# Two expert chunks of a loop pass loaded as 112 rows and twice 8 rows

## The chip, the cores and the metric

The kernel runs on one core of a Trainium2 chip. The metric is the device time of one execution in microseconds (us). A core has a matrix engine (TensorE, PE in the profile; its weight loads are PEld), VectorE (DVE), ScalarE (ACT), GpSimd (POOL) and SyncE (SP, which here issues nearly all loads), and 16 DMA engines that move data between the chip's memory and the core's on-chip memory of 128 partitions.

## The reference, cut to what matters

Two blocks work on 256 tokens of width 1024 in float32. The first has attention, retention, attention to a memory, and at its end a mixture of 32 experts; the second has two layers, each with a feed-forward part, token mixers and another feed-forward part. The change touches how the experts' weights are loaded:

```
def expert_block(args):
    toks, e = args
    xb = t_pad[toks]
    return (jax.nn.silu(xb @ w1[e]) * (xb @ w3[e])) @ w2[e]
```

Every expert has three matrices of 1024x512, 6 MB in all. Which tokens go to which expert is data, but the kernel streams the weights of all 32 experts in a fixed order.

## The kernel before, in words

The experts' weights come as 192 chunks of 1 MB: 128 rows of 8192 bytes, one for each partition. An expert is six chunks: four for the gate and up matrices, two for the down matrix. Four experts make a team, a team is served in one turn of 24 chunks (`TURN`), and two turns make a pass over 48 chunks. The first pass is written out (two turns, with `prev` equal to None); the others are a loop, `Fori(0, last_pair)` on SP at L2075 and on PE at L719. Eight teams of four experts make four passes, so the loop runs three times here.

The chunks go to slots of 8192 bytes per partition in one large on-chip buffer, the tile `ring` (and, for some slots, `more`). `expert_place` (L452) gives the slot of the j-th chunk and how many times it has been filled; in the loop sixteen slots are used in rotation, three fills of each per pass. Every slot has a semaphore `e_land[s]`; a load of a slot increments it by 16 when it has fully landed.

- SP (L2075 to L2078): for each of the 48 chunks of a pass it waits on `e_used`, which PE increments with the last matmul on a chunk, so that the slot is free, and then issues one load, in `expert_chunk` (L2042 to L2047).
- PE: `chunk_of` (L636) waits until the slot's semaphore has reached the count of its fills so far, and `turn` (L661) then runs the matmuls of the chunk: at L683 those of the gate and up matrices, at L702 those of the down matrix, with a transpose at L692 between. At the end of a turn L712 scatters the team's result. ACT (L753, L757, L760) and DVE (L868, L727) work on what lies between.
- Behind the loop SP goes on in `layer_loads` (L930) with the weights of the first feed-forward part of the second block, in tiles of 128 rows of 12288 bytes (tile memory `ring` again, input `in_wf`). For the first eight tiles, L943 waits until PE is through with the slots that the tile overwrites, L938 until the tile two before has landed, and L939 issues the load.
- ACT copies tile 0 and tile 1 at L974 (`whu`) as they land, in this order, then casts the transposed tokens (L1256), and PE starts the feed-forward part at L1183 when that is there.

All these loads are issued on one queue (q1 in the profile), in the order of the program.

Of the kernel before, what the change touches and what calls it, by code (L numbers as in the profile page):

```python
# [30 lines left out]
ESLOTS = 16  # L31
# [32 lines left out]
TURN = 6 * TEAM  # L64
# [32 lines left out]
def build(nc, d_x, d_mem, d_w1, d_we, d_wf, d_w2, d_cT1, d_row1, d_wr, d_cT2, d_row2, d_ln, d_tab, d_bias, d_out):  # L97
    ctx = ExitStack()
    with ctx:
# [42 lines left out]
        slot = [ring[:, s * CH:(s + 1) * CH] for s in range(SLOTS)]  # L142
# [67 lines left out]
        def block2(n):  # L210
            return n + 12 if n < 4 else n - 4 if n < 16 else n
# [15 lines left out]
        def sem(name):  # L227
            return ctx.enter_context(nc.semaphore(name))
# [15 lines left out]
        e_land = [sem(f"e_land{i}") for i in range(ESLOTS + EXTRA)]  # L244
# [126 lines left out]
        def head_rows(T, blk, first, n):  # L371
            return [T[first:first + n, blk, tok(i)] for i in range(NT)], T[first:first + n, blk, :]

        units1 = []
        for h in range(AH):
            rows = 64 * (h % 2)
            q, _ = head_rows(qkT, h // 2, rows, 64)
# [10 lines left out]
        for h in range(4):  # L388
            at_q, kv = [0, 2, 1, 3][h], h // 2
            q, _ = head_rows(qkT2, block2(at_q // 2), 64 * (at_q % 2), 64)  # L390
# [4 lines left out]
        for n in range(8):  # L395
            h, m = n // 2, n % 2
            q, _ = head_rows(qkT2, block2(3 + 2 * (n // 4)), 32 * (n % 4), 32)
# [4 lines left out]
        for h in range(4):  # L402
            at_q, kv = [0, 2, 1, 3][h], h // 2
            q, _ = head_rows(qkT2, block2(8 + at_q // 2), 64 * (at_q % 2), 64)
# [4 lines left out]
        for h in range(BH):  # L409
            q, _ = head_rows(qkT2, block2(10 + h), 0, BQ)  # L410
# [41 lines left out]
        def expert_place(j):  # L452

            if ESLOTS <= j < ESLOTS + EXTRA:
                return j, 1
            r = j if j < ESLOTS else j - EXTRA
            return e_slot[r % ESLOTS], r // ESLOTS + 1
        dense_slot = [(D_AT + c) % SLOTS for c in range(DENSE2)]
        OUT_ORDER = (0, 3, 2, 1)
        BANKS_W = (6, 0, 1, 2)  # L460
# [149 lines left out]
        def pe_moe(pe, tokens):  # L610
# [25 lines left out]
            def chunk_of(prev, t, j):  # L636

                n = t * TURN + j
                if prev is None:
                    s, fills = expert_place(n)  # L640
                    pe.wait_ge(e_land[s], fills * 16)
                else:
                    s, fills = expert_place(2 * TURN + n)
                    pe.wait_ge(e_land[s], (prev * (2 * TURN // ESLOTS) + fills) * 16)
                return slot[s].rearrange("p (k q n) -> p k q n", k=2, q=4)

            def weights_T(it):
# [13 lines left out]
            def turn(prev, t):  # L661
# [5 lines left out]
                for e, part in TEAM_ORDER:  # L667
                    if part == "u":
                        for c in range(4):
                            if e == 0:  # L670
                                if c == 1:
                                    pe.wait_ge(n_ok, 2)
                                    gather(it, 2)
                                if c == 2:
                                    gather(it, 3)
                                pe.wait_ge(m_xg, it * 4 + (c + 1))
                                if c == 2:
                                    weights_T(it)
                            w = chunk_of(prev, t, j)
                            for kk in range(2):  # L680
                                k = 2 * c + kk
                                for q in range(4):
                                    ins = pe.matmul(bank[4 + e % 2][q * CAP:(q + 1) * CAP, 0:2 * P],  # L683
                                                    xg[:, k, e * CAP:(e + 1) * CAP], w[:, kk, q],
                                                    start=(k == 0), stop=(k == KD - 1), skip_group_check=True)
                            ins.then_inc(e_used, 1)
                            j += 1
                        continue
# [8 lines left out]
                    for c in range(2):  # L697
                        w = chunk_of(prev, t, j)
                        for kk in range(2):
                            k = 2 * c + kk  # L700
                            for q in range(4):
                                ins = pe.matmul(bank[6][q * CAP:(q + 1) * CAP, 0:2 * P],  # L702
                                                hTe[:, e % 2, k * CAP:(k + 1) * CAP], w[:, kk, q],
                                                start=(k == 0), stop=(k == 3), skip_group_check=True)
                        ins.then_inc(e_used, 1)
                        j += 1
# [223 lines left out]
        def layer_loads(sp, last_pair):  # L930
            for p in range(2):
                sp.sem_inc(f_land[p], 16)
            for l in range(LAYERS):
                for f in range(2):
# [6 lines left out]
                    for v in range(FSLOTS):  # L941
                        if g == 0:
                            sp.wait_ge(e_used, last_pair * (2 * TURN) + max(  # L943
                                j + 1 for j in range(2 * TURN) if expert_place(2 * TURN + j)[0] in chunks_in(v)))
                        elif f == 0 and last_tile[(v + RING0) % FSLOTS] >= FT - 2:
                            sp.wait_ge(f_dn, g * (FT + 1))
                        elif f == 0:
                            sp.wait_ge(wl_ok, g * FFN_W + (2 * last_tile[(v + RING0) % FSLOTS] + 2))
                        else:
                            sp.wait_ge(d_used, l * DENSE2 + (DENSE1 + 1 + max(last_dense[s] for s in chunks_in(v))))  # L950
                        tile(v, v % 2)
# [1049 lines left out]
        def _(sp):  # L2001
# [24 lines left out]
            for t in (before, ones, iota, rel, desc, rope):  # L2026
                n = int(np.prod(t.shape[1:]))
# [14 lines left out]
            def expert_chunk(pair, j, place):  # L2042

                e, c = TEAM_CHUNKS[j % TURN]
                src = d_we[((pair % (TEAMS // 2)) * 2 * TEAM + (j // TURN * TEAM + e)) * 6 + c]
                s, _ = expert_place(place)
                sp.dma_start(slot[s], src).then_inc(e_land[s], 16)  # L2047

            by_slot = {expert_place(j)[0]: j for j in range(ESLOTS + EXTRA)}
            for free in (12, 13, 0, 1, 2, 3, 10, 11, 14, 15, 4, 16, 17, 5, 6, 8, 7, 9, 18, 19, 20):  # L2050
                if free < SLOTS1:
                    sp.wait_ge(d_used, DENSE1 - SLOTS1 + free + 1)
                elif free < SLOTS1 + 2:
                    sp.wait_ge(d_used, DENSE1 - 1 + free - SLOTS1)
                elif free < SLOTS:
                    sp.wait_ge(d_used, V1[-1] + 1)
                elif free < SLOTS + 2:
                    sp.wait_ge(o_ok, AH)
                elif free < ESLOTS:
                    sp.wait_ge(o_ok, UNITS1)  # L2060
                elif free < ESLOTS + 2:
                    sp.wait_ge(t_ps, 34)
                elif free == ESLOTS + 2:
                    sp.wait_ge(d_used, DENSE1)
                elif free == ESLOTS + 3:
                    sp.wait_ge(sumsq, 4)
                else:
                    sp.wait_ge(r_ps, 1)
                expert_chunk(0, by_slot[free], by_slot[free])
            used = 2 * TURN  # L2070
            for j in range(ESLOTS + EXTRA, used):
                sp.wait_ge(e_used, j - ESLOTS - EXTRA + 1 if j < 2 * ESLOTS + EXTRA else j - ESLOTS + 1)
                expert_chunk(0, j, j)
            last_pair = load_pairs(sp)
            with sp.Fori(0, last_pair) as prev:  # L2075
                for j in range(used):
                    sp.wait_ge(e_used, prev * used + (used - ESLOTS + j + 1))
                    expert_chunk(prev + 1, j, used + j)  # L2078
# [1078 lines left out]
```

## Time and profile before

| | |
|---|---|
| median of 3 runs | 1750.41 us |
| the three runs | 1749.85, 1750.41, 1752.44 us |
| the profiled execution's own time | 1750.45 us |
| its span, first to last instruction | 1748.7 us |
| mean granted TensorE clock, share of full speed | 0.946 |
| PE busy | 92% of the span |
| chain that ended last | PE 64%, DMA 11%, SP's queue 9% |

The span is what the trace shows; the device time is 1.75 us longer than it. Times in the trace count from the first instruction. The page cuts the span into 40 slices of 43.7 us; the expert stage lies from about 265 to 703 us, slices 7 to 16. "DMA share" is the mean busy share of the 16 DMA engines. It can exceed 1 a little, because a packet's recorded time overlaps the next one's by some nanoseconds, and by much in a very short window, where a packet counts with its whole time in the window in which it starts.

### The profile page before, as it was taken

To read this page: it belongs to the slowest core of one execution; us is meant where nothing else is said; L and a number is where in the kernel's file an instruction comes from. 1 tells how busy PE (TensorE), PEld (TensorE's weight loads), DVE (VectorE), ACT (ScalarE), POOL (GpSimd) and SP (SyncE) were. 2 spreads that over 40 slices of the span, in tenths; PEclk is the share of its full clock that TensorE was granted. 3 is DMA by queue.
4 is the path that set the end of the run, shared out by engine and by line. 5 is a ranking of instruction groups with operands and counts; after the bars stand their busy time and mean duration, and the time that the engine had idled before them with its cause. 6 is when DMAs were issued, how large, how long until landed. Compare 5 with 4: busy or idle time off the path is not lost.

```text
span 1748.7 us, 27045 instructions
## 1 busy us (share of the span) xinstructions
PE 1609.7 (92%) x10486; PEld 1219.6 (70%) x10497; DVE 957.6 (55%) x1493; ACT 622.5 (36%) x961; POOL 226.6 (13%) x241
## 2 busy tenths in 40 slices
PE   8999999777777776999999999999999999999998
PEld 6788985333323332788887788888888887788886
DVE  5675543111111110677776767677767766677767
ACT  5464431100010000443443643444344443653332
POOL 0232110000000000100133321001110133411000
PEclk9999999888767877999999999999999999999999
DMA  9515489999999999955445055533854534055511
GB/s 396 195 63 169 172 338 386 426 426 427 424 427 426 425 426 427 369 213 190 175 176 193 1 222 199 180 108 133 330 181 168 216 127 186 25 220 191 195 43 49
DMA packets 61100, 421.47 MB, mean 241 GB/s; under 512 B 7024, under 2 KB 16080, under 8 KB 17360
## 3 DMA queue, kind: packets, MB, share of 16 engines
q1 hardware_dynamic: 59280, 409.13, 59.7%
q10 hardware_dynamic: 1728, 11.03, 1.7%
q8 instruction: 68, 1.11, 0.2%
q14 instruction: 24, 0.20, 0.0%
HBM read 419.08 MB, written 1.05 MB: 240 GB/s over the span
## 4 chain that ended last, share of the span: by engine, by line
PE 64%; DMA 11%; SPq 9%; DVE 6%; issue 4%; POOL 3%; ACT 2%; DVEq 0%; ACTq 0%; POOLq 0%
PE bank L1162 17%; PE bank L1205 12%; DMA ring<-in_we 9%; SPq L2047 9%; PE bank L1164 9%; PE bank L2198 6%; PE bank L2224 2%; PE bank L2127 2%; PE bank L683 2%; PE bank L1545 2%; POOL x L1056 2%; DMA ring<-in_wf 2%; PE bank L1192 1%; PE bank L1183 1%; PE bank L1151 1%
## 5 line engine op out<-in xcount | busy, mean ns | idle before, releaser
L1162 PE MATMUL bank<-xhl,whu 128*128 128x512 f32 x1280 | 451.8, 396 | 0.0
L1164 PE MATMUL bank<-xhl,wlu 128*128 128x256 f32 x1280 | 357.5, 279 | 0.0
L1162 PEld LDWEIGHTS bank<-xhl,whu 128*128 128x128 f32 x1280 | 240.3, 188 | 57.8
L1164 PEld LDWEIGHTS bank<-xhl,wlu 128*128 128x128 f32 x1280 | 241.1, 188 | 3.3
L979 DVE TENSOR_TENSOR wlu<-ring,whu 128x2048 fp32r<-128x2048 f32 x84 | 192.5, 2292 | 43.9 <-ACT whu L974 43.9
L974 ACT ACTIVATE whu<-ring 128x2048 fp32r (+1 forms) x88 | 167.2, 1902 | 3.5 <-DMA ring<-in_wf 3.5
L979 DVE TENSOR_TENSOR wld<-ring,whd 128x1024 fp32r<-128x1024 f32 x80 | 98.6, 1233 | 113.4 <-ACT whd L974 113.4
L683 PE MATMUL bank<-ring,xg 128*32 128x256 f32 x1424 | 115.0, 466 | 39.1 <-DMA ring<-in_we 39.1
L974 ACT ACTIVATE whd<-ring 128x1024 fp32r (+1 forms) x80 | 84.8, 1060 | 128.5 <-PE bank L1205 128.5
L1272 ACT ACTIVATE sg<-sg 128x256 f32<-128x256 f32 x80 | 33.5, 418 | 265.8 <-DVE sg L1351 265.8
L683 PEld LDWEIGHTS bank<-ring,xg 128*32 128x32 f32 x1424 | 46.2, 126 | 99.4 <-DMA ring<-in_we 68.1
L2198 PE MATMUL bank<-ring_r,xTh 128*128 128x512 f32 x384 | 109.8, 397 | 4.6 <-DVE ring_r L514 2.5
L868 DVE TENSOR_TENSOR hmid<-hact,bank 128x128 f32<-128x128 f32 x32 | 9.2, 288 | 186.1 <-ACT hact L753 186.1
L702 PE MATMUL bank<-ring,hTe 128*32 128x256 f32 x832 | 76.4, 505 | 31.9 <-DMA ring<-in_we 21.6
L987 POOL TENSOR_TENSOR wlu<-ring,whu 128x512 fp32r<-128x512 f32 x16 | 21.2, 1355 | 586.3 <-ACT whu L974 556.1
L727 DVE COPY yg<-bank 32x256 f32<-32x256 f32 x64 | 27.2, 424 | 122.1 <-PE bank L702 121.6
L1205 PE MATMUL bank<-whd,hh 128*128 128x512 f32 x288 | 91.2, 398 | 0.0
L1205 PE MATMUL bank<-whd,hl 128*128 128x512 f32 x288 | 91.0, 397 | 0.0
L1205 PE MATMUL bank<-wld,hh 128*128 128x512 f32 x288 | 90.7, 396 | 0.0
L1056 POOL TENSOR_TENSOR x<-x,ln 128x512 f32<-128x512 f32 x40 | 63.5, 1600 | 204.5 <-DVE wlu L979 192.0
L2198 PEld LDWEIGHTS bank<-ring_r,xTh 128*128 128x128 f32 x384 | 71.3, 188 | 22.5 <-issue 3.2
L514 DVE TENSOR_TENSOR ring_r<-ring,ring_r 128x2048 fp32r<-128x2048 f32 x26 | 59.6, 2291 | 49.4 <-ACT ring_r L506 49.4
(349 smaller groups left out, 2777.4 us busy)
## 6 DMA issues: line engine op xcount, KB each, us to landing
ring<-in_we SPq DMA_DIRECT2D x141, 1024.0 KB, 26.9
ring<-in_wf SPq DMA_DIRECT2D x88, 1536.0 KB, 6.4
ring<-in_w SPq DMA_DIRECT2D x52, 1024.0 KB, 5.0
more<-in_we SPq DMA_DIRECT2D x51, 1024.0 KB, 25.8
ring<-in_w SPq DMA_DIRECT2D x32, 256.0 KB, 3.7
ln<-in_ln ACTq DMA_DIRECT2D x6, 1024.0 KB, 5.9
bias<-in_bias ACTq DMA_DIRECT2D x2, 2048.0 KB, 7.3
bias<-in_bias SPq DMA_DIRECT2D x1, 2048.0 KB, 20.4
```

What stands on the lines that cost most here:

```text
L514: ins = eng.tensor_tensor(slot_r[n % SLOTS1][:, part], slot[n % SLOTS1][:, part], high1[n % 2][:, part].bitcast(F32), ALU.subtract)
L683: ins = pe.matmul(bank[4 + e % 2][q * CAP:(q + 1) * CAP, 0:2 * P], xg[:, k, e * CAP:(e + 1) * CAP], w[:, kk, q], start=(k == 0), stop=(k = ...
L702: ins = pe.matmul(bank[6][q * CAP:(q + 1) * CAP, 0:2 * P], hTe[:, e % 2, k * CAP:(k + 1) * CAP], w[:, kk, q], start=(k == 0), stop=(k == 3 ...
L974: act.activation(dst[:], ring[:, bass.ds(ring_tile(t) + first, D if down else 2 * D)], ACT.Copy).then_inc(wh_ok, 1)
L979: eng.tensor_tensor(dst[:], ring[:, bass.ds(ring_tile(t) + first, D if down else 2 * D)], src[:].bitcast(F32), ALU.subtract).then_inc(done, 1)
L1056: ins = pool.tensor_tensor(x[:, i, cols], x[:, i, cols], ln[:, n // 4, cols], (ALU.mult, ALU.add)[n // 4])
L1162: pe.matmul(into[:].rearrange("p (a s) -> p a s", a=2), whu[p][:, cols], xhl[:, :, k], start=(k == 0), stop=False, skip_group_check=True)
L1164: ins = pe.matmul(into[:, 0:S], wlu[p][:, cols], xh[:, k], start=False, stop=(k == KD - 1), skip_group_check=True)
L1205: ins = pe.matmul(bank[2 * i + c][:], v[p][:, tok(i)], w[p][:, c * 512:(c + 1) * 512], start=False, stop=False, skip_group_check=True)
L1545: ins = pe.matmul(bank[BANKS_W[2 * i + h]][:], v[:, tok(i)], w[:, kk, h * 512:(h + 1) * 512], start=(pos == 0 and kk == 0 and m == 0), sto ...
L2047: sp.dma_start(slot[s], src).then_inc(e_land[s], 16)
L2198: ins = pe.matmul(bank[banks[2 * i + h]][:], v[:, k, tok(i)], w[:, kk, h * 512:(h + 1) * 512], start=(k == 0 and m == 0), stop=(k == KD - ...
```

## The change

In the loop, and there only, chunks number 22 and 46 of a pass are loaded by three instructions in place of one: rows 0 to 111, rows 112 to 119 and rows 120 to 127. Each of the three increments the slot's semaphore by 16, so such a fill counts 48. The wait of PE is adapted: `turn_lands` gives, for chunk n of a loop pass, the slot, how much its semaphore rises per pass, and the count for the first pass. Chunk 22 is the first of the two down chunks of the last expert of the first turn, and chunk 46 the same of the second turn. The same bytes are loaded to the same places in the same order of chunks.

```diff
+        UNEVEN = (22, 46)
+
+        def extra_land(j):
+
+            return 32 if j in UNEVEN else 0
+
+        def turn_lands(j):
+
+            s, fills = expert_place(2 * TURN + j)
+            same = [q for q in range(2 * TURN) if expert_place(2 * TURN + q)[0] == s]
+            return s, 16 * len(same) + sum(map(extra_land, same)), fills * 16 + sum(extra_land(q) for q in same if q <= j)
+
...
                 else:
-                    s, fills = expert_place(2 * TURN + n)
-                    pe.wait_ge(e_land[s], (prev * (2 * TURN // ESLOTS) + fills) * 16)
+                    s, every, first_at = turn_lands(n)
+                    pe.wait_ge(e_land[s], prev * every + first_at)
...
                 s, _ = expert_place(place)
-                sp.dma_start(slot[s], src).then_inc(e_land[s], 16)
+                if place >= 2 * TURN and j in UNEVEN:
+                    sp.dma_start(slot[s][0:112], src[0:112]).then_inc(e_land[s], 16)
+                    for r in (112, 120):
+                        sp.dma_start(slot[s][r:r + 8], src[r:r + 8]).then_inc(e_land[s], 16)
+                else:
+                    sp.dma_start(slot[s], src).then_inc(e_land[s], 16)
```

## Rows read from the trace of the kernel before

**Rows 1.** Busy tenths in 40 slices of the span, from the page.
```profile
PE   8999999777777776999999999999999999999998
...
PEclk9999999888767877999999999999999999999999
DMA  9515489999999999955445055533854534055511
GB/s 396 195 63 169 172 338 386 426 426 427 424 427 426 425 426 427 369 213 190 175 176 193 1 222 199 180 108 133 330 181 168 216 127 186 25 220 191 195 43 49
```

**Rows 2.** Stretches: us, PE busy, PEld, DVE, ACT, POOL, clock, DMA share, GB/s.
```profile
320.00:440.00 120.00, 86.44 (x872) 38.35 (x876) 15.11 (x45) 10.99 (x34) 0.00 (x0) 0.80 1.01 426
560.00:680.00 120.00, 88.92 (x868) 37.78 (x860) 15.07 (x44) 11.07 (x34) 0.00 (x0) 0.77 1.01 426
730.00:800.00 70.00, 70.00 (x366) 59.29 (x365) 50.04 (x61) 26.69 (x25) 0.00 (x0) 1.00 0.67 246
```

**Rows 3.** Waits from 320 to 700: who for whom, total us, times, longest.
```profile
PEld bank L683 <- DMA ring<-in_we: 68.1, 43, 2.8
...
PE bank L683 <- DMA ring<-in_we: 39.1, 41, 2.3
```

**Rows 4.** The DMA view of the stretch from 285 to 700 us.
```profile
q1 hardware_dynamic: 24115, 176.20, 100.7%
q8 instruction: 30, 0.49, 0.4%
...
ring<-in_we SPq DMA_DIRECT2D x120, 1024.0 KB, 27.1
more<-in_we SPq DMA_DIRECT2D x38, 1024.0 KB, 25.9
```

**Rows 5.** Chain that ended last, 640 to 712 us: start, length, what.
```profile
647.39 27.70 DMA ring<-in_we
675.09 0.04 issue
675.13 1.83 PE bank L683 x16
...
678.96 28.19 DMA ring<-in_wf
707.15 0.02 issue
707.17 1.92 ACT whu L974
709.09 0.03 issue
709.11 0.61 ACT xhl L1256
709.72 0.14 issue
709.85 5.98 PE bank L1183 x48
```

**Rows 6.** DMA share of all 16 engines in short stretches around 700 us.
```profile
699.00:699.50 0.50, 0.00 (x0) 0.00 (x0) 0.00 (x0) 0.00 (x0) 0.00 (x0) 1.00 1.06 451
699.50:700.00 0.50, 0.09 (x4) 0.10 (x8) 0.00 (x0) 0.00 (x0) 0.00 (x0) 1.00 0.81 344
700.00:700.50 0.50, 0.50 (x12) 0.32 (x16) 0.00 (x0) 0.00 (x0) 0.00 (x0) 1.00 0.81 344
700.50:701.00 0.50, 0.48 (x12) 0.00 (x0) 0.00 (x0) 0.00 (x0) 0.00 (x0) 1.00 0.52 221
...
703.50:704.00 0.50, 0.50 (x3) 0.26 (x2) 0.38 (x1) 0.47 (x1) 0.00 (x0) 1.00 0.52 221
```

**Rows 7.** ACT's timeline where the first two feed-forward tiles have landed.
```profile
703.52 1.91 ACT L974 ACTIVATE whu<-ring 128x2048 fp32r<-128x2048 f32 x1 [1.72 <-DMA ring<-in_wf]
```

**Rows 8.** The line of the expert loads, and SP's timeline of two tile issues.
```profile
L2047 SPq FUSED_REGOPS  x144: 46/46/139, 320.0 to 670.5; - x144
L2047 SPq DMA_DIRECT2D ring<-in_we x141: 340/1892/5898, 198.9 to 670.6; - x141
...
703.58 8.29 SPq L939 DMA_DIRECT2D ring<-in_wf  x3
761.09 0.34 SPq L957 DMA_DIRECT2D ring<-in_wf  x1
```

**Rows 9.** Packets that start within 0.2 us after two issues, DMA view.
```profile
DMA packets 9, 0.11 MB, mean 553 GB/s; under 512 B 0, under 2 KB 0, under 8 KB 0
...
DMA packets 10, 0.12 MB, mean 614 GB/s; under 512 B 0, under 2 KB 0, under 8 KB 0
```

## The prediction

> **What bounds the kernel now.** I read the page's slices first. PE is busy nine tenths nearly everywhere, but in slices 8 to 16 it falls to six or seven tenths while the DMA engines stand at nine and move 424 to 427 GB/s [rows 1]. That is the expert stage. The stretches say the same: DMA share 1.01 and 426 GB/s, PE busy 86 to 89 of 120 us [rows 2]. The waits name what PE lacks there: its weight loads at L683 wait 68.1 us for landings of `in_we`, its matmuls 39.1 us [rows 3]. Between 285 and 700 us the queue carries 158 chunks, each landing 26 to 27 us after its issue [rows 4]. A chunk of 1.049 MB at 426 GB/s takes 2.46 us, so some eleven are in flight: what counts is when the DMA engines get to the end of the queue, not when SP issues. The chain that ended last goes the same way: a chunk's 27.7 us, PE on it, then the 28.19 us of a feed-forward tile behind the experts in the same queue, ACT's copy and cast, and PE's L1183 at 709.85 us [rows 5]. From there PE is busy without a gap (70.00 of 70.00 us between 730 and 800, at clock 1.00) and the DMA share is down to 0.67 [rows 2]. So what the stage gives or loses up to 709.85 us goes one to one to the end, and nothing else the loads do matters much.
>
> **The finer reading** is that the 16 engines don't finish together. A landing needs all of them. Near 700 us the last expert chunk and tiles 0 and 1 are in the queue, and tile 2 is issued only when tile 0 has fully landed (L938). The DMA share is 1.06 until 699.5, falls to 0.81, and stands at 0.52 from 700.5 to 704 [rows 6]. Half of the engines have nothing left, while the other half still works: it ends tile 0 at 703.5 (ACT's copy starts at 703.52 [rows 7]) and tile 1 at 707.15 [rows 5]. The early half was through with tile 1 at about 700.0, the middle of the fall. It is thus 7.1 us ahead of the slowest late one, and the landings, PE and the end go by the late half. What makes half of them late I can show in part: 30 fetches of instructions of 16 KB went through the same engines in that stretch, with 0.4% of 16 engines for 415 us [rows 4], 27 us. Spread over eight engines these are 3.3 us each, about half of the 7.1.
>
> **The change part by part.** All is priced against the profiled execution, 1750.45 us (span 1748.7 plus 1.75), which is 0.04 us from the median of 1750.41.
>
> (a) *Rows taken from engines.* Every engine has 8 of a chunk's 128 rows. A row takes 2.46 / 8 = 0.308 us on its engine. Loading 112 rows leaves 7 on each of the sixteen. Two pieces of 8 rows must then put 16 rows somewhere. If a piece uses eight engines, and both pieces the same eight, these have 9 rows and the other eight 7. No DMA of this trace shows a piece of 8 rows, so I bound it. At one end the pieces fall on the early half: the late half has one row less per uneven chunk. At the other end they fall on the late half and it has one more. SP's register instruction runs 144 times from 320 us on [rows 8], three passes of 48, so there are 6 uneven chunks: -1.85 or +1.85 us. Wider ends (all rows on one engine; an even spread) are rivals below.
>
> (b) *Which half.* One view bears on it. Tile 2 is issued at 703.58 us, when one half is idle, and 10 packets start from 0.92 to 1.12 us behind the issue; the busy half, at one 12 KB packet in 0.46 us (2.46 x 1.5 / 8), starts 3 or 4 of these, so 6 or 7 of the idle eight are at work by then. At 761.09 us a tile is issued with all sixteen idle [rows 8], and between 0.91 and 1.11 us 9 of the sixteen start [rows 9] (first row 762.0 to 762.2, second row 704.5 to 704.7). Were engines served in no order, about 4.5 of the idle eight would have started; were the idle half the last served, about one. It looks like the half that is served first. A piece for eight engines would naturally take the first ones. This is two launches and an inference, so it moves my odds and proves nothing.
>
> The Trainium skill says this outright: the page "DMA: Bandwidth & Descriptors", section "Why a DMA increments its semaphore by 16 and not by 1", has a load use the largest number of engines up to 16 that divides its rows, the lowest-numbered ones. By that 112 rows use 16 engines and 8 rows the lowest 8; with (b) the sum would be -1.85 us. No row here numbers the engines.
>
> (c) *Does the whole -1.85 arrive?* The early half gets 1.85 us later, so its lead shrinks from 7.1 by 3.7 to 3.4 us. It stays ahead, so the late half still sets each landing, and nothing takes its place. Tile 0, tile 1, the transposes and L1183 all hang on landings of the same queue and move together. PE's sequence before L1183 (last chunk, scatter, transposes) starts from a landing as well. I take all of it: -1.85.
>
> (d) *Twelve more loads on SP.* Issues of L2047 take 0.34 to 5.90 us, 1.89 in the middle [rows 8]; an issue of 0.34 us is one into a free queue, as at 761.09. Twelve cost SP 4.1 us at the least, 22.7 at the middle value and 71 at the most. I take zero for the end: SP runs 26 to 27 us ahead of the landings [rows 4], two issues of one chunk can eat at most 11.8 us of this, and the queue refills before the next uneven chunk 24 chunks (59 us) later. If that cover were gone, the 22.7 us would count. What stands behind the two issues on SP is the next chunk's wait and load, with the same cover. POOL and ACT issue nothing here.
>
> (e) *Semaphore writes and PE's waits.* Each extra piece adds writes of a few bytes on the early half only, which has 3.4 us to spare. PE's wait is a register instruction as before; even 0.05 us more for the 18 waits on the two slots would be 0.9 us, and PE idles before most of them for a landing [rows 3]. Zero, at most +0.9.
>
> Sum: 1750.45 - 1.85 = **1748.6 us**, 0.11% less. A measurement of this kernel can tell about 0.2%, 3.5 us, from no change (the runs of before lie 2.6 us apart), so the likeliest verdict is the same.
>
> **The rivals.** *The pieces fall on the late half* (place: the queues of that half; price 6 x 0.308; it decides if the first-served eight are the late ones). 1750.45 + 1.85 = 1752.3, slower than before. For it: only that (b) is thin. 0.14.
>
> *Nothing moves.* If the rows of a piece are cut so that all 16 engines share them, each engine again has 8 rows' worth: 1750.4. The same if tile 1's time were set by PE instead; against that stands the wait of ACT for the landing [rows 7]. 0.09.
>
> *All 8 rows of a piece on one engine.* It gets 7 + 16 rows in place of 8, 15 x 6 x 0.308 = 27.7 us more, less its lead of 7.1 if it is an early one: 1771. Against it: large loads here spread over all engines. 0.03.
>
> *The small pieces cost by the piece.* If SP or the queue spends 1.9 us on each whatever its size and the cover of (d) doesn't hold, 12 x 1.89 = 22.7 us: 1773. Against it: eleven chunks in flight. 0.04. The Trainium skill's page "DMA: Bandwidth & Descriptors", section "Rules for kernel authors", speaks for this one: small transfers are to be coalesced, and under 64 KB one pays mostly overhead (a piece is 64 KB); its fixed cost of about 2.0 us (section "Anatomy of one DMA") would give an estimate of 24 us.
>
> *A larger gain*, over 3.5 us, if late landings also cost elsewhere, as in SP's or PE's waits behind them: 0.04. The forecast itself has 0.66.
>
> **How the numbers follow.** The forecast alone gives 1747.0 to 1750.2, the spread of the runs around 1748.6. To reach 8 in 10 the range must take in "nothing moves" and the late half at 1752.3: 1746.8 to 1752.5. Faster by over 0.2% (under 1746.9): the larger gain and the edge of the forecast, 0.11. Slower by over 0.2% (over 1753.9): both costly rivals and the edge of the late-half one, 0.09. Same: 0.80.
>
> **What the profile after would show.** Right: under `in_we` six loads of 112 rows and twelve small ones; around 698 us the half-idle stretch (share near 0.5) shorter by about 3.7 us, and L1183 at about 708.0. Rival late half: the half-idle stretch longer by 3.7 us, L1183 at 711.7. Nothing moves: L1183 at 709.85. Small pieces by the piece: DMA share under 1 behind the uneven chunks, landings well under 26 us. The prediction is wrong if L1183 doesn't move by 1.85 us, or if it does and the end doesn't follow.

## The result and the profile after

The changed kernel takes 1790.76 us (median of 6 runs, 1783.9 to 1794.25), the kernel before beside it 1751.5 (6 runs, 1749.85 to 1755.32): ratio 1.0219, 95% interval 1.0201 to 1.0238. It is slower by 39 us, where 1.85 us less were forecast. The profiled execution took 1790.11 us with a span of 1788.3, against 1748.7 before.

The page first, its slices. Those of before are [rows 1].

```profile
PE   9999999767757757699999999999999999999998
PEclk9999999877767678799999999999999999999999
DMA  9515499999999999885436126534654445055511
GB/s 397 194 48 180 174 372 378 426 389 422 387 367 426 367 362 426 285 314 189 166 145 230 71 68 274 180 136 165 262 202 177 165 187 189 1 225 187 187 59 47
DMA packets 61196, 421.47 MB, mean 236 GB/s; under 512 B 7120, under 2 KB 16176, under 8 KB 17456
```

The DMA engines stand at nine in the expert stage as before, but five of its slices move only 362 to 389 GB/s where every one moved 424 or more. So the engines are as busy and do less. The bytes are the same 421.47 MB. Before, the page counted 61100 packets, 7024 of them under 512 B: there are 96 more now, all of them tiny. In e1 below, twelve additional loads of 128 rows leave 192 more (7216 in all), 16 each, one for every engine. Here twelve additional loads leave 96, 8 each: a piece of 8 rows uses eight engines, as part (a) of the prediction supposed.

Where the time went stands in the stretches (the columns are those of [rows 2]).

```profile
380.00:394.00 14.00, 9.40 (x92) 2.85 (x84) 0.85 (x2) 0.75 (x2) 0.00 (x0) 0.62 1.01 425
394.00:404.00 10.00, 4.74 (x38) 1.62 (x34) 1.14 (x3) 1.58 (x5) 0.00 (x0) 0.50 1.01 243
404.00:420.00 16.00, 14.44 (x97) 7.26 (x97) 3.42 (x11) 0.74 (x2) 0.00 (x0) 0.71 1.01 424
320.00:440.00 120.00, 86.82 (x843) 38.12 (x843) 14.95 (x44) 10.54 (x33) 0.00 (x0) 0.74 1.01 411
440.00:560.00 120.00, 83.46 (x796) 37.72 (x796) 14.21 (x42) 10.32 (x32) 0.00 (x0) 0.73 1.01 389
560.00:680.00 120.00, 78.51 (x710) 32.21 (x710) 13.16 (x39) 9.86 (x30) 0.00 (x0) 0.70 1.01 380
```

There is a hole of about 10 us, from 394 to 404. The rate drops from 425 to 243 GB/s and comes back, and all the while the share is 1.01. Five more follow, one for each uneven chunk. The DMA views of the first two stretches count the packets.

```profile
DMA packets 818, 5.95 MB, mean 425 GB/s; under 512 B 93, under 2 KB 93, under 8 KB 93
...
DMA packets 351, 2.43 MB, mean 243 GB/s; under 512 B 54, under 2 KB 54, under 8 KB 54
...
q1 hardware_dynamic: 351, 2.43, 101.5%
```

In 14 us 16 engines carried 725 large packets, 0.31 us of an engine each. In the 10 us of the hole they carried 297, at full share, which is 0.54 us each. If eight engines had been slowed and the others had waited idle, the share would have dropped. It didn't: nearly all engines spent longer on each packet. The trace's packet records say the same one by one: from 380 to 394 us all but one of 724 packets of 8192 bytes took 0.309 us, and of the 162 that start from 396 to 402 us none took less than 0.475.

PE's granted clock is 0.50 in the hole. PE mostly waits there, and the DMA engines are full all the while, so a slower PE is not what holds the loads up.

The uneven chunk of this hole was issued at 371 us, 23 us earlier. SP's timeline shows its three loads, and line L2062 gives all twelve small ones.

```profile
371.38 0.36 SPq L2060 DMA_DIRECT2D ring<-in_we  x1
371.92 5.95 SPq L2062 DMA_DIRECT2D ring<-in_we  x2
...
L2062 SPq DMA_DIRECT2D ring<-in_we x12: 295/1987/5415, 371.9 to 705.7; - x12
```

The queue is some 26 us long [rows 4], so the hole sits where the queue reaches the uneven chunk, not where SP issues it. The issues of the small loads last 1.99 us in the middle, as other issues into this full queue do ([rows 8], 1.89), and the page still has the loads of `in_we` landing 27.1 us after their issue in the middle. SP is not what is late. What is late is the landing: of the waits, here 320 to 740 us, matmuls and weight loads at L714 (L702 before) have grown most. They waited 21.6 and 28.7 us for landings of `in_we` before.

```profile
PEld bank L695 <- DMA ring<-in_we: 65.9, 40, 3.7
...
PE bank L714 <- DMA ring<-in_we: 53.6, 35, 3.8
PEld bank L714 <- DMA ring<-in_we: 50.4, 27, 3.9
PE bank L695 <- DMA ring<-in_we: 38.7, 40, 3.1
```

The chain that ended last now ends its expert part with chunk 47, the one behind the last uneven chunk and held up in the same queue:

```profile
708.82 30.58 DMA ring<-in_we
...
739.44 1.92 PE bank L714 x16
...
749.55 5.47 PE bank L1195 x45
```

L1195 is L1183 of before. It starts at 749.55 us in place of 709.85 [rows 5], 39.7 us later, and the span is 39.6 us longer. All of the loss arises before this point and nothing is won back behind it; from 750 on PE is busy without a gap as before. Tiles 0 and 1 have landed when ACT's copies of them start, at 703.52 [rows 7] and 707.17 [rows 5] before, and both are 39.5 us later:

```profile
743.06 1.91 ACT L986 ACTIVATE whu<-ring 128x2048 fp32r<-128x2048 f32 x1 [0.91 <-DMA ring<-in_wf]
746.71 1.91 ACT L986 ACTIVATE whu<-ring 128x2048 fp32r<-128x2048 f32 x1 [1.74 <-DMA ring<-in_wf]
```

Shared over six uneven chunks the loss is 6.6 us each, for a chunk that took 2.46. The engines don't lose alike. By the packet records the packets of 8192 bytes between 270 and 760 us took 35.3 us per engine beyond 0.309 us each, before 2.6: the mean engine lost 32.7 us, and the last one, for which every landing waits, 39.5. Shortly before tile 0 has landed only two of sixteen still work (a share of 0.12):

```profile
739.00:742.00 3.00, 1.87 (x16) 0.60 (x16) 0.60 (x2) 0.60 (x2) 0.00 (x0) 0.65 0.12 49
```

### The profile page after: what moved, and what is told of

Read it like the earlier page. It is cut to its first block, busy times and chain, and to the rows that moved or that the text cites. A ratio compares the mean times of both kernels' runs of the same rounds, so it can differ in the third digit from the quotient of the medians.

```text
span 1788.3 us, 27087 instructions
## 1 busy us (share of the span) xinstructions
PE 1615.8 (90%) x10486; PEld 1223.6 (68%) x10497; DVE 957.8 (54%) x1493; ACT 622.1 (35%) x961; POOL 226.4 (13%) x241
## 2 busy tenths in 40 slices
DMA packets 61196, 421.47 MB, mean 236 GB/s; under 512 B 7120, under 2 KB 16176, under 8 KB 17456
## 4 chain that ended last, share of the span: by engine, by line
PE 63%; DMA 11%; SPq 10%; DVE 6%; issue 4%; POOL 3%; ACT 2%; DVEq 0%; ACTq 0%; POOLq 0%
PE bank L1174 17%; PE bank L1217 11%; SPq L2064 9%; PE bank L1176 8%; DMA ring<-in_we 7%; PE bank L2215 6%; DMA more<-in_we 4%; PE bank L2241 2%; PE bank L2144 2%; PE bank L1557 2%; PE bank L695 2%; POOL x L1068 2%; PE bank L1204 1%; PE bank L1195 1%; PE bank L1163 1%
## 5 line engine op out<-in xcount | busy, mean ns | idle before, releaser
L695 PE MATMUL bank<-ring,xg 128*32 128x256 f32 x1424 | 110.5, 453 | 38.7 <-DMA ring<-in_we 38.7
L714 PE MATMUL bank<-ring,hTe 128*32 128x256 f32 x832 | 81.7, 532 | 58.8 <-DMA ring<-in_we 53.6
L714 PEld LDWEIGHTS bank<-ring,hTe 128*32 128x32 f32 x832 | 29.1, 139 | 99.1 <-DMA ring<-in_we 50.4
## 6 DMA issues: line engine op xcount, KB each, us to landing
ring<-in_we SPq DMA_DIRECT2D x135, 1024.0 KB, 27.1
```

Of the source, the lines that this page charges most:

```text
L714: ins = pe.matmul(bank[6][q * CAP:(q + 1) * CAP, 0:2 * P], hTe[:, e % 2, k * CAP:(k + 1) * CAP], w[:, kk, q], start=(k == 0), stop=(k == 3 ...
```

## The experiments

The first theories were these. **N**: loads cost by their number, three for one. **B**: the balance of rows over engines is worse than I took it. **P**: it matters which rows a load writes. P comes in two forms: P1 blames the load of 112 rows, P2 the pieces of 8 neighbouring rows. **H**, for e11, says that only a crowded queue is disturbed, and that loads by themselves go by their bytes. Each experiment but e11 touches chunks 22 and 46 alone, or adds loads right behind them. The diffs of e1, e2, e3, e6, e12 and e13 are against the changed kernel, the others against the kernel before; `...` marks lines left out. The kernel before, run beside them, had medians of 1750.85 us (for e1, e2, e3 and e6, 15 runs) and 1752.15 (e7 to e10, 7 runs, 1749.34 to 1753.04), and 1751.28 in one run (e11 to e13).

### e1: three loads of all 128 rows

```diff
-                    sp.dma_start(slot[s][0:112], src[0:112]).then_inc(e_land[s], 16)
-                    for r in (112, 120):
-                        sp.dma_start(slot[s][r:r + 8], src[r:r + 8]).then_inc(e_land[s], 16)
+                    for a, b in ((0, 1024), (1024, 1536), (1536, 2048)):
+                        sp.dma_start(slot[s][:, a:b], src[:, a:b]).then_inc(e_land[s], 16)
```

> Chunks 22 and 46 of a loop pass are loaded in three instructions as in the change, but cut by columns (1024, 512 and 512 of 2048) with all 128 rows in each. Theory P (places: the cut by rows takes engines off their own share of partitions, and several then write through the same port): no slow packets, end within 3 us of before, about 1751. Theory N (number: three loads and 48 counts on one semaphore in place of one load cost by themselves): about as slow as the change, 1785 to 1790. Theory B (balance: the two small pieces overload one half of the engines): within 3 us of before too, since the cut by columns keeps all 16 engines equal.

Measured: 1752.78 us (1750.73 to 1753.82), ratio 1.0007, interval 0.9997 to 1.0016. The same. It has as many loads, as much semaphore work and the same waits as the change, and no hole:

```profile
394.00:404.00 10.00, 5.67 (x67) 2.27 (x68) 2.59 (x8) 1.76 (x5) 0.00 (x0) 0.97 1.02 424
```

N falls. Terms (d) and (e) of the prediction, additional issues and semaphore writes, are too small to be measured. It is the cut by rows that costs.

### e2: 112 and 16 rows

```diff
-            return 32 if j in UNEVEN else 0
+            return 16 if j in UNEVEN else 0
...
-                    sp.dma_start(slot[s][0:112], src[0:112]).then_inc(e_land[s], 16)
-                    for r in (112, 120):
-                        sp.dma_start(slot[s][r:r + 8], src[r:r + 8]).then_inc(e_land[s], 16)
+                    for a, b in ((0, 112), (112, 128)):
+                        sp.dma_start(slot[s][a:b], src[a:b]).then_inc(e_land[s], 16)
```

> The same chunks as 112 rows and one piece of 16 rows, which all 16 engines can share; no piece of 8 rows is left. Theory P1 (the 112 rows do it, 7 consecutive rows to an engine): dips of the DMA rate as in the change, 4 to 7 us lost at each of the six chunks, end 1775 to 1790. Theory P2 (the pieces of 8 rows do it, eight engines on a few neighbouring partitions): little is left, end under 1760. Theory B: no loss, 1751.

Measured: 1792.68 us (one run), 41.8 over before. The page counts 7120 packets under 512 B, 96 more than before, so each load of 16 rows uses all sixteen engines. There is no piece of 8 rows here, and the time is that of the change, so neither the pieces of 8 nor the balance that they make is the main cause: B falls as such.

### e3: halves, rows 0 to 63 and 64 to 127

```diff
-            return 32 if j in UNEVEN else 0
+            return 16 if j in UNEVEN else 0
...
-                    sp.dma_start(slot[s][0:112], src[0:112]).then_inc(e_land[s], 16)
-                    for r in (112, 120):
-                        sp.dma_start(slot[s][r:r + 8], src[r:r + 8]).then_inc(e_land[s], 16)
+                    for a, b in ((0, 64), (64, 128)):
+                        sp.dma_start(slot[s][a:b], src[a:b]).then_inc(e_land[s], 16)
```

> The same chunks as two halves of 64 rows, 4 rows to each of the 16 engines. Theory P: 64 neighbouring partitions reach only half of the ports, so while a half is written the engines share them by two and packets take about twice 309 ns: at least 2.5 us lost for each of the six chunks, end over 1765. Theories N and B: no loss for balance; N gives two thirds or half of the change's 39 us.

Measured: 1783.57 us (one run), 32.7 over before, 5.5 us a chunk. 64 and 64 is as even a cut as there is, and still dear. Both show the hole, e2 in the first row and e3 in the second:

```profile
394.00:404.00 10.00, 4.02 (x41) 1.66 (x45) 0.85 (x2) 1.02 (x3) 0.00 (x0) 0.62 0.99 286
```

```profile
394.00:404.00 10.00, 3.90 (x38) 1.47 (x41) 1.14 (x3) 1.41 (x5) 0.00 (x0) 0.65 1.01 283
```

### e12: halves again, every second row

The question that remains behind e3 is whether a load of 64 rows is dear, or these 64 rows are. This one writes the even rows with one load and the odd rows with the other.

```diff
-            return 32 if j in UNEVEN else 0
+            return 16 if j in UNEVEN else 0
...
-                    sp.dma_start(slot[s][0:112], src[0:112]).then_inc(e_land[s], 16)
-                    for r in (112, 120):
-                        sp.dma_start(slot[s][r:r + 8], src[r:r + 8]).then_inc(e_land[s], 16)
+                    for r in (0, 1):
+                        sp.dma_start(slot[s][r:127 + r:2], src[r:127 + r:2]).then_inc(e_land[s], 16)
```

> Chunks 22 and 46 as two loads of 64 rows, but even rows and odd rows instead of the upper and the lower half. The number of loads, rows and bytes is that of the 64 and 64 run (1783.6). Theory P: each load now reaches all ports, so engines crowd less, end between 1755 and 1775. If only the count of rows per engine matters: 1783 again.

Measured: 1751.51 us, the kernel before beside it 1751.28 (one run each). Expected were 1755 to 1775; it costs nothing at all. The stretch has its full rate:

```profile
394.00:404.00 10.00, 6.88 (x66) 2.31 (x65) 1.93 (x5) 2.04 (x6) 0.00 (x0) 0.67 1.01 428
```

e3 and e12 load the same bytes with as many loads of as many rows, and lie 32 us apart. Which rows go together in a load decides. That is P. (The two also group the source rows differently; e7, e8 and e11 leave the source alone and show the same.)

### e13: only one of the two chunks uneven

```diff
-        UNEVEN = (22, 46)
+        UNEVEN = (22,)
```

> The change with chunk 22 alone cut up (three chunks in all instead of six). Each uneven chunk costs by itself, 39 / 6 = 6.5 us: end near 1770. If the cost came from the first of them or from the adapted waits: 1785 or more.

Measured: 1770.66 us (one run), 19.4 over before, 6.5 for each of three chunks where the change has 6.6 for each of six. The costs add up chunk by chunk. No one place in the pass is to blame.

### e9 and e10: the 112 rows and the 16 rows alone, as spare loads

These and the next two kernels keep all chunks of before whole and add loads behind chunks 22 and 46. They fill slot 20, which is not in use then, have a semaphore of their own, and nobody reads what they bring. PE waits for nothing new. SP waits, ahead of the next spare loads and once in `layer_loads`, until the last ones have landed.

```diff
...
+            SPARE = {22: [(0, 112, 1)], 46: [(0, 112, 1)]}
...
+                    if j in SPARE:
+                        rows = SPARE[j]
+                        sp.wait_ge(spare_in, prev * 48 + 32 * (j == 46) + 16 * (j == 22))
+                        for n_, (a, b, step) in enumerate(rows):
+                            sp.dma_start(slot[20][a:b:step], d_we[0][0:(b - a + step - 1) // step]).then_inc(spare_in, 16)
...
```

> The kernel before plus one spare load of 112 rows behind chunks 22 and 46, no piece of 8 rows anywhere. The bytes alone are 7 rows more per engine, 6 x 7 x 0.308 = 12.9 us, end 1763. Theory P1: slow packets as in the change, 20 to 35 us more on top, 1785 to 1800. Theory P2: 1763 and packets of 309 ns.

Measured: 1805.25 us (one run), 53.1 over before, and more than P1's 1785 to 1800. The bytes account for 6 x 0.875 x 2.46 = 12.9 us of it. The other 40.2 us, 6.7 a load, are as much as the change lost in all (39.3). Its hole:

```profile
394.00:404.00 10.00, 5.10 (x54) 2.08 (x50) 1.14 (x3) 1.52 (x5) 0.00 (x0) 0.67 1.02 289
```

e10 has `SPARE = {22: [(0, 16, 1)], 46: [(32, 48, 1)]}` in its place.

> The kernel before plus one spare load of 16 neighbouring rows behind chunks 22 and 46; the bytes alone are 1 row more per engine, 1.85 us, end 1752.3. Theory P1: that and nothing more. Theory P2 (small pieces on few partitions): some us more, 1755 to 1765.

Measured: 1759.04 us (one run), 6.9 over before, of which bytes are 1.85. Sixteen neighbouring rows cost 0.8 us a load beyond their bytes. 1759 lies in the range of P2, not in P1's "nothing more": the small neighbouring pieces cost something too. But it is an eighth of what a load of 112 rows costs, so that one is the dear one of the change's loads.

### e7 and e8: four pieces of 8 rows, apart or neighbouring

Both have four spare pieces of 8 rows behind each of the two chunks, 24 in all. In e7 a piece takes every fourth of 32 rows, in e8 eight neighbours. Both read the same source rows.

```diff
+            SPARE = {22: [(0, 29, 4), (1, 30, 4), (2, 31, 4), (3, 32, 4)], 46: [(32, 61, 4), (33, 62, 4), (34, 63, 4), (35, 64, 4)]}
```

```diff
+            SPARE = {22: [(0, 8, 1), (8, 16, 1), (16, 24, 1), (24, 32, 1)], 46: [(32, 40, 1), (40, 48, 1), (48, 56, 1), (56, 64, 1)]}
```

> The kernel before, all chunks whole, plus four spare loads of 8 rows of 8192 bytes behind chunks 22 and 46 of each loop pass, into a slot that nobody reads then; a piece takes every fourth of 32 rows (partitions r, r+4, ... r+28 of the lower 64), so that each row falls to another group of four partitions. 24 rows more for the eight engines of such pieces, 24 x 0.308 = 7.4 us. Theory P: no slow packets. If those eight are the early half, which is 7.1 us ahead, the end moves by 0 to 2.5 us (1751 to 1753); if they are the late half, by 7.4 (1758). Theory N (by the piece): 24 pieces cost as much as the change's 12 or more, over 1780.

> As the run before, with the same sources and sizes, but each piece goes to 8 neighbouring partitions. Only the place of the rows differs. Theory P2 (pieces of 8 neighbouring rows clog): slow packets behind each uneven chunk, end clearly over that of the run before, by 5 to 20 us. Theory P1 (only the 112 rows do it) and the reading that the source in memory is what collides: the same as the run before within 2 us.

Measured: e7 1760.69 us (1760.69 to 1760.71, ratio 1.0052, interval 1.0035 to 1.0069), nearer to the late half's 1758 than to the early half's 1751 to 1753; e8 1773.44 (1771.86 to 1773.77, ratio 1.0123, interval 1.0106 to 1.014). The two differ in nothing but the rows that they write, by 12.8 us, 0.53 a piece. That is P2's range again: P1 by itself asked for no difference. e8 has the hole, if a shallow one, in the DMA view of 396 to 402:

```profile
DMA packets 306, 2.01 MB, mean 335 GB/s; under 512 B 61, under 2 KB 61, under 8 KB 61
...
q1 hardware_dynamic: 306, 2.01, 102.2%
```

e7 has none (426 GB/s there). It is the clean measure of the balance, then, and term (b) can be read from it. ACT's timeline has the landings of tiles 0 and 1:

```profile
710.56 1.91 ACT L977 ACTIVATE whu<-ring 128x2048 fp32r<-128x2048 f32 x1 [0.85 <-DMA ring<-in_wf]
...
714.23 1.91 ACT L977 ACTIVATE whu<-ring 128x2048 fp32r<-128x2048 f32 x1 [1.76 <-DMA ring<-in_wf]
```

Before they were 703.52 [rows 7] and 707.17 [rows 5]: both are 7.0 to 7.1 us later. 24 pieces put one row each on each of eight engines, 24 x 0.308 = 7.4 us. Had the eight been the early half, 7.1 us ahead, the landings would have moved by 0.3. They moved by nearly the whole 7.4, so at least one of the slowest engines is among the eight. How many, the share in the stretches before the tiles land shows:

```profile
700.00:705.00 5.00, 2.40 (x33) 1.05 (x33) 0.85 (x2) 1.02 (x3) 0.00 (x0) 1.00 0.89 374
...
706.00:707.00 1.00, 0.05 (x4) 0.05 (x8) 0.00 (x0) 0.00 (x0) 0.00 (x0) 0.50 0.54 229
707.00:708.00 1.00, 1.00 (x12) 0.54 (x16) 0.00 (x0) 0.00 (x0) 0.00 (x0) 0.50 0.35 147
708.00:709.00 1.00, 0.88 (x12) 0.00 (x1) 0.05 (x1) 0.05 (x1) 0.00 (x0) 0.50 0.15 61
709.00:710.00 1.00, 0.04 (x1) 0.07 (x1) 0.81 (x2) 0.70 (x2) 0.00 (x0) 0.50 0.12 49
710.00:711.00 1.00, 1.00 (x2) 0.48 (x3) 0.00 (x0) 0.44 (x1) 0.00 (x0) 0.50 0.12 49
```

Before, the share stood at 0.52 until the first tile had landed [rows 6], eight of sixteen engines. Now it is 0.89 from 700 to 705, some fourteen of sixteen, and steps down to 0.12, two of sixteen. An early engine with 7.4 us more ends where a late one without ends, and only late ones with 7.4 us more are left: two. The eight engines of a piece are six early ones and two late ones. The span of e7 grew by 10.2 us. The 3 us that the landings don't account for are PE's: it does the last scatter (L712, here L713) at a granted clock of 0.50, and before at 1.00. The first row is of before, the second of e7:

```profile
702.06 3.67 PE L712 MATMUL bank<-yg,sT 128*128 128x512 f32 x8 [1.08 <-DVE yg L727]
```

```profile
709.96 6.65 PE L713 MATMUL bank<-yg,sT 128*128 128x512 f32 x8 [1.08 <-DVE yg L728]
```

In the changed kernel this scatter takes 3.67 us as before, so nothing of its loss is of this kind.

### e6: can the cut be made without the crowding?

Part of the columns of a chunk is loaded in pieces of 8 rows that stand four apart. By count it gives eight engines 9 rows' worth of a chunk and the other eight 7, as the change meant to.

```diff
-            return 32 if j in UNEVEN else 0
+            return 256 if j in UNEVEN else 0
...
-                    sp.dma_start(slot[s][0:112], src[0:112]).then_inc(e_land[s], 16)
-                    for r in (112, 120):
-                        sp.dma_start(slot[s][r:r + 8], src[r:r + 8]).then_inc(e_land[s], 16)
+                    sp.dma_start(slot[s][:, 0:1792], src[:, 0:1792]).then_inc(e_land[s], 16)
+                    for r in (0, 1, 2, 3, 32, 33, 34, 35, 64, 65, 66, 67, 96, 97, 98, 99):
+                        sp.dma_start(slot[s][r:r + 29:4, 1792:2048], src[r:r + 29:4, 1792:2048]).then_inc(e_land[s], 16)
```

> The imbalance of the change without its cut of the 128 rows: columns 0 to 1791 of all 128 rows in one load, and columns 1792 to 2047 in 16 pieces of 8 rows, each piece taking every fourth row of 32. If pieces of 8 rows run on eight engines, these get one row's worth (8 KB) per chunk more and the other eight one less, as the change meant. My forecast's balance with P: few slow packets, end 1748.6 if the pieces go to the early half, 1752 if to the late half. Theory B against the forecast: 1785 as in the change. Theory N: 17 loads in place of one, worse than the change, over 1800.

Measured: 1765.17 us (1763.2 to 1765.67, ratio 1.0076, interval 1.0062 to 1.0089). None of the expected values. Small pieces of 1 KB rows, two late engines among the eight, and a rate of 388 GB/s in the stretch where e1 has 424 come together in it, and I can't part them.

### e11: loads by themselves, on idle engines

All of the above happens in a full queue. e11 puts 22 groups of four loads ahead of the program, each group waiting for the one before, in two rounds of eleven shapes.

```diff
+            sp.dma_start(slot[8][0:64:1], d_we[0][0:64]).then_inc(spare_in, 16)
+            sp.dma_start(slot[9][0:64:1], d_we[1][0:64]).then_inc(spare_in, 16)
+            sp.dma_start(slot[10][0:64:1], d_we[2][0:64]).then_inc(spare_in, 16)
+            sp.dma_start(slot[11][0:64:1], d_we[3][0:64]).then_inc(spare_in, 16)
+            sp.wait_ge(spare_in, 256)
+            sp.dma_start(slot[8][0:127:2], d_we[0][0:64]).then_inc(spare_in, 16)
...
```

> The kernel before with 22 groups of loads ahead of everything else, on otherwise idle DMA engines; SP waits behind each group until all of it has landed, and only the times of the groups count. Rows are 8192 bytes, the source always begins at row 0 of a chunk. Eleven kinds, each twice: four loads of 128 rows; four of 112; 128, 112, 128, 128; four of rows 0 to 63; four of every second row; four of 16 neighbouring rows; four of every eighth row; four of 8 neighbouring; four of every fourth of 32 rows; 128, 8 neighbouring, 128, 128; 128, 16 neighbouring, 128, 128. By bytes per engine at 0.308 us a row, plus some 2.5 us from issue to first and last byte: 12.4, 11.1, 12.0, 7.4, 7.4, 3.7, 3.7, 3.7, 3.7, 10.2, 10.2 us. Theory P: the kinds whose engines share a port take more, four of 112 by 5 us or more, four of rows 0 to 63 about twice the bytes' part (12), 16 neighbouring rows more than every eighth row, 8 neighbouring more than every fourth of 32, 128-112-128-128 by 3 us or more. Theory H (only a crowded queue of many chunks does it): all by their bytes.

The whole took 1970.01 us, which says nothing; the groups are read from SP's timeline, the first issue of a group against that of the next.

```profile
0.73 0.39 SPq L2016 DMA_DIRECT2D ring<-in_we  x1
...
12.87 0.35 SPq L2021 DMA_DIRECT2D ring<-in_we  x1
...
29.72 0.36 SPq L2026 DMA_DIRECT2D ring<-in_we  x1
...
43.16 0.62 SPq L2031 DMA_DIRECT2D ring<-in_we  x1
...
55.96 0.51 SPq L2036 DMA_DIRECT2D ring<-in_we  x1
...
64.50 0.35 SPq L2041 DMA_DIRECT2D ring<-in_we  x1
...
70.82 0.57 SPq L2046 DMA_DIRECT2D ring<-in_we  x1
...
75.58 0.35 SPq L2051 DMA_DIRECT2D ring<-in_we  x1
...
81.90 0.75 SPq L2056 DMA_DIRECT2D ring<-in_we  x1
...
86.67 0.37 SPq L2061 DMA_DIRECT2D ring<-in_we  x1
...
97.66 0.34 SPq L2066 DMA_DIRECT2D ring<-in_we  x1
...
109.31 0.34 SPq L2071 DMA_DIRECT2D ring<-in_we  x1
```

| group of four loads | first round, us | second round, us |
|---|---|---|
| 128 rows | 12.1 | 12.5 |
| rows 0 to 111 | 16.9 | 16.0 |
| 128, 112, 128, 128 | 13.4 | 13.4 |
| rows 0 to 63 | 12.8 | 12.8 |
| every second of 128 | 8.5 | 8.6 |
| 16 neighbours | 6.3 | 6.5 |
| every eighth of 128 | 4.8 | 4.6 |
| 8 neighbours | 6.3 | 6.2 |
| every fourth of 32 | 4.8 | 4.8 |
| 128, 8 neighbours, 128, 128 | 11.0 | 11.1 |
| 128, 16 neighbours, 128, 128 | 11.7 | 11.5 |

Seven eighths of the bytes take a third longer than the whole, and 64 neighbours take longer than 128 rows. Rows 4 and 5, 6 and 7, 8 and 9 of the table are pairs with the same source and the same number of rows, and only the rows written differ: 4.3, 1.7 and 1.5 us. So the place alone costs, also without a queue, and H falls. But it doesn't explain the size. One load of 112 rows between whole ones takes 13.4 us here; by its bytes it would be 0.31 us less than the four whole loads' 12.1 and 12.5, so 1.2 to 1.6 us are beyond its bytes, against 6.7 in the full queue of e9. Nor do the shapes rank alike: sixteen neighbouring rows in that place (the last row) take 1.1 to 1.7 us beyond their bytes, as much as 112, and only 0.8 in the full queue of e10.

## Why the prediction was wrong

**The step that failed** is the sentence in (a) that a row takes 0.308 us on its engine, whatever load it belongs to. All the bounds of (a) and most rivals count rows by engine at this price. It holds for loads of all 128 rows, the only ones that the trace of before had in this stage, and for the even and the odd rows of e12. In a load of 112 neighbouring rows it doesn't: the packets of all engines took 0.54 us in place of 0.31 while it passed. I had noted that no DMA of that trace shows a piece of 8 rows and looked for what eight rows could cost, but the 112 rows were priced as seven eighths of a chunk without a bound of their own. No row of before showed a load of 112 rows either. Its price is 6.7 us beyond its bytes (e9), and six of them come to 40.2 us, where the change lost 39.3.

**What makes it dear** is where the rows lie (e3 against e12, e7 against e8, the pairs of e11). That much the runs show. Why it matters is not shown.
By its other steps: **what bounds the kernel** was right. The stage's landings went one to one to the end: 39.5 us at tiles 0 and 1, 39.7 at L1195, 39.6 in the span. **(a), eight engines for a piece**: right, by the 96 tiny writes, and e7's 7.0 of 7.4 us. **(b), the early half**: wrong. Six early and two late engines take the pieces. The start counts of [rows 8, 9] had pointed to "mostly early", which is so, but a landing needs all engines, and one late engine among the eight is enough to turn the sign. **(c), the whole -1.85 arrives**: without ground, since it rested on (b). Had rows cost what I took, the sum would have been the rival's +1.85. That rival, the late half, is right about who decides and is 38.5 us short. **(d) and (e)**: nothing at the end, as said; e1 has both and is unchanged. Only that the writes of (e) fall on the early half alone is wrong, with (b). **The costly rivals** had sizes of 21 to 23 us and the wrong mechanism: small loads don't cost by the piece (24 more of them cost 8.5 us in e7, where 1.89 each would be 45), and no engine got all rows. The 2.0 us of the page that the prediction names there stand in the Trainium skill for loads that GpSimd issues; here SP does. What I had named as the mark of "by the piece", a share under 1 and shorter landings, didn't appear; the mark of the real cause, a full share at a lower rate, I hadn't named.

**What stays open**: whether it is the ports; why a load of 112 rows costs four to six times as much in a full queue (6.7 us beyond its bytes) as on idle engines (1.2 to 1.6); what e6's 14 us are made of; and why the holes' price doesn't add over kinds (112 rows 40.2 and 16 rows 5.0 as spare loads, together 45, but 41.8 in e2). No version here beats the kernel before. The gain that a cut could have had is small: at most half of the 7.1 us between the halves, by estimate.

## What to carry to other kernels

A load's price is not its bytes: if a load must be cut up, cut it by columns (e1, free) or by interleaved rows (e12, free), and not into blocks of neighbouring rows while the queue is full (5.5 to 7 us a chunk here). Price every shape that the trace doesn't show, the large one too, and not only the small one that looks odd. When the DMA share is full and GB/s falls, divide the packets into the time: if each has become longer, look for what they collide at, not for who issues late.

## What was not expected of the hardware

- One chunk loaded as 112 and twice 8 rows in a queue of whole chunks brought the DMA engines from 425 to 243 GB/s for some 10 us, with a share of 1.01. One spare load of 112 rows alone brought them to 289 (e9).
- Loads of 64 rows: rows 0 to 63 took as long as 128 (12.8 us for four against 12.1), every second row 8.5.
- The engines that serve 8-row loads include two of the eight that are up to 7.1 us late at the end of the expert stage.
